# State-space layer on one core: 8 to 8.5 input tiles per group in place of 10, five gate tiles multiplied on at the end, decay rows over a group's x chunks, transposed sums

## The reference

```python
def ssd_chunked(x, dt, a, bm, cm, init_state):
    ...
    acs = jnp.cumsum(dtc * a.reshape(SSD_GROUPS, r), axis=2)
    seg = acs[:, :, :, None] - acs[:, :, None, :]
    lmat = jnp.exp(jnp.where(lower, seg, -jnp.inf))
    cb = jnp.einsum('bcign,bcjgn->bcijg', cc, bc)
    wmat = cb[..., None] * lmat * dtc[:, :, None]
    y_diag = jnp.einsum('bcijgr,bcjgrp->bcigrp', wmat, xc)
    ...
    chunk_states = jnp.einsum('bcjgn,bcjgrp->bcgrpn', bc, xw)
    ...
    y_off = jnp.einsum('bcign,bcgrpn->bcigrp', cc, starts) * jnp.exp(acs)[..., None]

def ssd_mixer(h, w_in, conv_w, conv_b, dt_bias, a_log, d_skip, norm_g, w_out, init_f=None, init_b=None):
    proj = h @ w_in
    z, xbc, dt = jnp.split(proj, [SSD_DI, SSD_DI + SSD_XBC_W], axis=-1)
    xbc = jax.nn.silu(dwconv_centered(xbc, conv_w, conv_b))
    ...
    y = y_f + jnp.flip(y_b, 1) + xs.astype(jnp.float32) * d_skip.astype(jnp.float32)[:, None]
    y = y.reshape(b, n, SSD_DI) * jax.nn.silu(z.astype(jnp.float32))
    y = rmsnorm(y, norm_g).astype(h.dtype)
    return y @ w_out, s_f, s_b
```

## Time and profile before

| | us |
|---|---|
| median of 3 runs | 1921.57 |
| lowest and highest | 1917.19, 1923.33 |
| profiled execution | 1917.99 |
| its span in the profile | 1916.2 |
| TensorE busy | 1830.8 |
| VectorE, ScalarE, GpSimdE busy | 999.6, 602.5, 1188.0 |
| TensorE busy from 1000 to 1050 us | 50.00 of 50 |
| from 1250 to 1300 us, granted clock 0.93 | 38.05 of 50 |
| from 1300 to 1350 us, granted clock 0.80 | 35.59 of 50 |

### The profile page before, as it was taken

The page is one execution under the profiler, slowest core; times in us unless marked ns, Lnnn a source line. Parts: engine busy times, 40 slices in busy tenths (PEclk is TensorE's granted clock), DMA queues, the critical chain, the costliest instruction groups (busy, mean ns, idle before and its releaser), DMA issues. The chain is left out here.

```text
span 1916.2 us, 33393 instructions
## 1 busy us (share of the span) xinstructions
PE 1830.8 (96%) x12837; PEld 1726.8 (90%) x12837; DVE 999.6 (52%) x1597; ACT 602.5 (31%) x1148; POOL 1188.0 (62%) x869
## 2 busy tenths in 40 slices
PE   6999999999999999989999999986999999999997
PEld 4888899999999999989898898965999999999997
DVE  4556654562256146373656756595436633661552
ACT  3344421220022012144566657473112200220221
POOL 2533466777777777846455454515787777777774
PEclk9999999999999999999999999997999999999999
DMA  9641164424243433534333333233222222222222
GB/s 342 198 136 38 32 223 151 157 75 155 67 164 92 139 102 115 166 92 135 99 111 111 99 111 99 67 100 110 67 78 66 77 76 67 77 77 72 71 61 82
DMA packets 256188, 208.65 MB, mean 109 GB/s; under 512 B 7353, under 2 KB 235742, under 8 KB 255454
## 3 DMA queue, kind: packets, MB, share of 16 engines
q1 hardware_dynamic: 255373, 204.69, 33.9%
q10 hardware_dynamic: 720, 2.62, 0.3%
HBM read 196.63 MB, written 10.67 MB: 108 GB/s over the span
## 5 line engine op out<-in xcount | busy, mean ns | idle before, releaser
L1002 POOL TENSOR_SCALAR w_hi<-raw 128x512 fp32r<-128x512 f32 (+1 forms) x432 | 641.0, 1501 | 706.7 <-PE ps L1036 527.2
L1006 POOL TENSOR_TENSOR w_lo<-raw,w_hi 128x512 fp32r<-128x512 f32 (+1 forms) x432 | 553.9, 1303 | 0.0
L1036 PE MATMUL ps<-h_hi,w_hi 128*128 128x324 f32 (+1 forms) x1432 | 343.8, 321 | 4.7 <-DVE h_lo L2392 3.1
L1036 PE MATMUL ps<-h_hi,w_lo 128*128 128x324 f32 (+1 forms) x1432 | 328.8, 311 | 0.0
L1036 PE MATMUL ps<-h_lo,w_hi 128*128 128x324 f32 (+1 forms) x1432 | 327.5, 310 | 0.0
L1036 PEld LDWEIGHTS ps<-h_hi,w_hi 128*128 128x128 f32 x1432 | 241.2, 190 | 20.7 <-issue 18.4
L1036 PEld LDWEIGHTS ps<-h_hi,w_lo 128*128 128x128 f32 x1432 | 240.5, 189 | 0.0
L1036 PEld LDWEIGHTS ps<-h_lo,w_hi 128*128 128x128 f32 x1432 | 240.3, 189 | 0.0
L2282 DVE SCALAR_TENSOR_TENSOR xT<-ps,mod,xT 128x128 f32 (+1 forms) x112 | 56.6, 547 | 270.9 <-PE ps L1036 265.3
L1036 PE MATMUL ps<-g_hi,w_hi 128*128 128x324 f32 (+1 forms) x816 | 188.7, 312 | 4.8 <-POOL w_lo L1006 3.2
L1036 PE MATMUL ps<-g_hi,w_lo 128*128 128x324 f32 (+1 forms) x816 | 187.2, 310 | 0.0
(11 more groups left out here) (355 smaller groups left out, 3113.7 us busy)
## 6 DMA issues: line engine op xcount, KB each, us to landing
raw<-in_ffn_w_up SPq DMA_DIRECT2D x88, 512.0 KB, 3.9
ada<-in_ada_w SPq DMA_DIRECT2D x40, 1024.0 KB, 6.5
raw<-in_ssd_w_in SPq DMA_DIRECT2D x40, 512.0 KB, 4.0
raw<-in_ffn_w_down SPq DMA_DIRECT2D x32, 512.0 KB, 3.9
R<-scr_acs SPq DMA_DIRECT2D x22, 512.0 KB, 5.3
raw<-in_att_w_in SPq DMA_DIRECT2D x16, 512.0 KB, 7.8
ada_att<-in_ada_w SPq DMA_DIRECT2D x8, 1024.0 KB, 8.3
raw<-in_ssd_w_out SPq DMA_DIRECT2D x16, 512.0 KB, 4.0
```

The source lines that it names most:

```text
L1002: nc.gpsimd.tensor_scalar(w_hi[j % 2][:, a_:b_, :], raw[j][:, a_:b_, :], 1.0, None, ALU.mult).then_inc(w_hi_done, 1)
L1006: ins = nc.gpsimd.tensor_tensor(w_lo[j % 2][:, a_:b_, :], raw[j][:, a_:b_, :], w_hi[j % 2][:, a_:b_, :].bitcast(F32), ALU.subtract)
L1036: ins = mm(out[:, cols], w[slot][:, k, :], x[:, cols], start=first and k == 0 and i == 0, stop=last and k == n - 1 and i == 2)
```

## The change

- **Tile order.** Groups 0 and 1 have 8 tiles (two z), group 2 has 9 (three z), group 3 has 10. The z tiles of rows 2, 3, 6, 7 and 11 stand at 35 to 39. Their rows of `yg` are set to 1 (five memsets in tile 3), the scan multiplies into them, and a new step `gate` on VectorE multiplies the SiLU of z, which ScalarE leaves in `cx`.
- **Scan places.** The b tiles are 0, 8, 16, 25 and the scans start at half tiles 14, 30, 47 and 64 (tiles 7, 15, 23.5 and 32).
- **End.** Chunks 0 to 3 of group 3 stand before the end of tile 39. Behind it follow `yd` of chunk 3, `yo` and `cb` of chunk 4, `yd` of chunk 4, then all out-projection pieces. `ynorm` is no longer spread through the scan.
- **Decay rows.** `R_last` lies over `x_tok[0]`, which group 2 has left, and its transfer waits for group 2 instead of tile 39.
- **Transposed sums.** The four matmuls at the end of `yd` are marked as transposes.
- **SyncE.** `LEAD` is 3. The store of `acs`, which SyncE waits for, now stands behind weight tile 7 where it stood behind tile 9. Two weight tiles of the out-projection are issued before the wait for the last `yd`.

```diff
+CONV_AT = (0, 8, 16, 25)
+SLOT_AT = (14, 30, 47, 64)
+Z_ROWS = ((0, 1), (4, 5), (8, 9, 10), (12, 13, 14, 15))
+Z_LATE = (2, 3, 6, 7, 11)
...
-        slots = [(b + 7 + i // 2, i % 2) for i in range(0, 40)]
+        slots = [divmod(SLOT_AT[g] + i, 2) for i in range(0, 40)]
...
-    return out
+        out += [ev for ev in after[k] if ev[0] != "yd"]
+    return out + end[:1] + [("yd", GROUPS - 1, 4)] + end[1:] + [("yout", GROUPS - 1, k) for k in range(12)]
...
-        R_last = at("R_last", [P, 2, GH, P], F32, aligned(h_at + 12 * WS * 4))[0]
+        R_last = x_tok[0][:, :, :].rearrange("p c n -> p (c n)")[:, 0:2 * GH * P].rearrange(
+            "p (a b c) -> p a b c", a=2, b=GH)
...
-                    sp.wait_ge(mm_done, T_E + 40)
+                    sp.wait_ge(*ssd_end(("yd", GROUPS - 2, CHUNKS - 1)))
+                    sp.wait_ge(st_done, CS_AT[("csf", GROUPS - 2, 3)] + 1)
...
-            LEAD = 5
+            LEAD = 3
...
-            sp.wait_ge(*ssd_end(("yd", 3, 4)))
-            sp.wait_ge(st_stored, 128)
-            sp.dma_start(xT[:, :, :], scr_x).then_inc(x_back, 16)
-            with sp.Fori(1, 4) as i:
+            for j in range(4):
+                if j == 2:
+                    sp.wait_ge(*ssd_end(("yd", 3, 4)))
+                    sp.wait_ge(st_stored, 128)
+                    sp.dma_start(xT[:, :, :], scr_x).then_inc(x_back, 16)
+                load(j, T_O + 4 + j, w_so[:, (j % 2) * 8:(j % 2) * 8 + 8, (2 + j // 2) * P:(3 + j // 2) * P])
+            with sp.Fori(2, 4) as i:
...
                         ins = mm(bank(b, P, q_ * P), y1[ev[2] % 2][:, q_ * P:(q_ + 1) * P], ident, start=False,
-                                 stop=q_ == 3, skip_group_check=True)
+                                 stop=q_ == 3, is_transpose=True, skip_group_check=True)
...
+                        if m in Z_LATE:
+                            dst = cx[:, :]
+                            if m != Z_LATE[0]:
+                                act.wait_ge(gated, Z_LATE.index(m))
+                        A_(dst, acc(e % 2), ACT.Silu).then_inc(acc_free_act, 1)
...
+                if kind == "gate":
+                    m = ev[2]
+                    dve.wait_ge(*acc_free(A_E + TILE_OF[("z", m)]))
+                    dve.wait_ge(*ssd_end(("yd", m // 4, 4)))
+                    tt(yg[:, m, :], yg[:, m, :], cx[:, :], ALU.mult).then_inc(gated, 1)
```

84 lines of the change are left out of this document (52 added, 32 removed).

## The result

The changed kernel takes 1947.63 us (median of four runs, 1945.96 to 1952.99) where the kernel before takes 1922.45 (four runs): a ratio of 1.0145, with a 95% interval of 1.0127 to 1.0163. It is slower, as forecast, but by 25 us where 15 were forecast: inside the range of 1908 to 1950, above the forecast's own of 1928 to 1944. The profiled execution took 1948.97 us, its span is 1947.2 us, its mean granted clock 0.973; before, these were 1917.99, 1916.2 and 0.985.

The account below looks back on a forecast made before the run. TensorE, busy 1830.8 of 1916.2 us, was taken as the bound. 1917.99 less 30.6 gained plus 48.2 added gave 1935.6, with half the 3.6 us offset about 1937 us; own range 1928 to 1944, wider range 1908 to 1950.

Parts of the forecast that it names:

- gain 3: Before the first regular out-projection tile: weights issued early save 2.2 of the 6.70 us wait.
- term 3: First `csb` of a group at tiles 15, 23 and 32 waits for VectorE's weighing: 4.7 us added in sum.
- Term 1: Half tiles 12.0 and 20.0: x transposes wait for a bank VectorE frees late, 7.2 us twice, 14.4 us added.
- Term 7: Low clock after the new waits of the x transposes: 2 us each, 6 us added together, bounds 0 and 9.
- term 6: Last chunk, between the last two `yd`: TensorE idle 5.1 us plus low clock 2.5, 7.6 us added.
- gain 1: Sums at the end of `yd` as transposes: 0.65 us saved 20 times, 13.1 us.
- Gain 2: Behind tile 39: the 5.39 us wait for `R_last` and the low clock behind it go, 8.5 us saved.
- Gain 4: The recurring bank waits of `cb` and `csf`, 3.8 and 3.0 us, are replaced by the added waits: 6.8 us saved.
- The rival in which each wait is at its floor: All added waits smallest, no low clock: 21.2 us added against 30.6 gained, 1910 us; chance 0.20.
- The rival of two passes: Sums in `yd` go through twice as before despite the transpose mark: 13.1 us more, 1950 us; chance 0.05.
- half and half: Bank waits some 4 us each, low clock behind only one: about 33 us added, 1920 to 1923 us; chance 0.17.
- the late tile 8: Weight tile 8 lands much later, behind other transfers: 1940 to 1943 us; chance 0.06.

Follow-up runs that it names:

- e3: The changed kernel with plain matmuls in place of transposes for the sums in `yd`: ratio 1.0197 to the kernel before.
- e1: The kernel before with only the sums at the end of `yd` marked as transposes: 1916.10 us, ratio 0.9979.
- e11: The changed kernel with another spacing, first group nine tiles long and group 2 eight: ratio 1.0176 to the kernel before.
- e2: The kernel before with only the last chunk's decay rows `R_last` laid over `x_tok[0]` and `ynorm`'s squares moved to `st_in`: ratio 0.9990.
- e12: The changed kernel with x transposes before `stT`, `acs` store and loads behind weight tile 9, first `csb` of groups 1 and 3 a half tile later: 1925.11 us, 1.0030.
- e4: The kernel before, old tile order, with transposed sums, decay rows over `x_tok[0]` and early loads of two out-projection weight tiles: 1915.34 us, ratio 0.9971.

## Why the prediction was right in sign and wrong in size

The sum was +17.6 us on the profiled execution; the stretch became 26.1 us longer. Taken apart into idle time, cheaper sums, and clock:

| | forecast | measured |
|---|---|---|
| idle time, net | +25.3 | +26.4 |
| transposed sums, busy time | -13.1 | -10.4 (e3) to -11.2 (e1) |
| low clock | +5.4 | +10.9 |

The forecast idle time is the added waits 1 to 6 and 8 without their low clock, 39.7, less the 5.39, 2.2 and 6.8 us of gains 2 to 4. The low clock measured is the busy time after less that of e1, 476.3 - 465.4: the same matmuls at different clocks. The forecast one is 6 + 2.5 - 3.1. Idle time and low clock are not quite separate costs, since where VectorE sets the pace the one takes from the other; their sum is what counts.

**The waits** were found at their places and nearly in their sizes (us):

| added | forecast | measured |
|---|---|---|
| 1. x transposes, twice | 14.4 | 13.3 |
| 2. the same at 28.1 and 29.0 | 5.3 | 5.4 (1.31 + 4.13) |
| 3. first `csb` of a group | 4.7 | 7.6 (3.95 + 0.80 + 2.82) |
| 4. half tiles 8.1, 16.1 | 4.7 | 4.7 |
| 5. weight tile 8 | 3.5 | 4.15 |
| 6. last chunk, without clock | 5.1 | 5.9 |
| 8. `yo` behind ScalarE | 2 | 1.4 |

These waits are 42.4 us where 39.7 were forecast, and the first wait for a split grew by 1.0 (gain 3 below). Against it, 2.8 us of short waits between 1267 and 1283 us in the kernel before went too, which no term had. So the net comes out 1.1 over the forecast.

Of term 3 the place at tile 32 was mis-sized, 0.5 us forecast for 2.82. Term 1 was right in its two legs as well: from the start of tile 10's convolution to the state update's end are 25.8 us (943.82 to 969.64) where the walk has 24.8, and TensorE's own work up to its request took about 1.7 us more than the walk's 17.6, in part by the low clock in it. The experiments took 1 (13.3 to 5.6 us), 3 (7.6 to 2.8) and 5 (to nothing) away and got that idle time back, so these causes are shown. Term 4 is shown for half tile 8.1 by e11, where it goes with a longer group. Terms 2, 6 and 8 have only their rows.

**What failed is the size of two terms.** Term 7, the low clock, was put at 2 us behind each of three long waits, term 6 had 2.5 us more, and the other waits had nothing. The trace shows it behind every one of the nine waits of 2.3 us or more ahead of the out-projection: the 10 us behind each read 0.82 to 0.84, after 2.34 us (921.07 and 1030.30) as after 4.15, 3.95 or 5.89. Eight of these waits are new and the ninth is that of term 6. A wait of 2.34 us cost about as much clock as one twice as long, so the number of waits was the thing to count, and the term came out twice as large. The profile of before had shown that short waits do it, in places that the walk did not read: the 10 us behind each of the three pairs of 1.28 and 0.99 us (949.38, 1059.00, 1168.61) read 0.83 to 0.85. One such row of before, from 1060 us on, reads 0.88, and this one, behind the pair a group earlier, 0.84:

```profile
950.00:960.00 10.00, 10.00 (x58) 9.14 (x56) 7.70 (x11) 2.71 (x4) 3.23 (x3) 0.84 0.18 54
```

And gain 1 was put at 0.65 us for each `yd`, as 1.09 less half of the 0.87 of an eight-transpose row (rows 3). A row of four transposes takes 0.66 us at full clock (980.36 in the changed kernel), not the 0.44 of the half. Over all 20 places the sums took 24.1 us before and 13.2 with transposes, that is 0.55 less each. Both errors go the same way, and with the waits' 1.1 they make 5.5 + 1.9 + 1.1 = 8.5 us, which is the miss in the stretch, 26.1 - 17.6. The profiled execution as a whole is 31.0 us longer; of the other 4.9, 2.8 lie ahead of the stretch, where kernels with the same work differ by as much, and 2.1 behind it, which no run explains.

**Gain 2** came true, but not by the part of the change that the expectation of e2 gave it to. The wait of 5.39 us stood before the `yd` of chunk 1. e2 shows that the place of the rows has no part in it: the row (rows 2) names VectorE's product as the releaser, and VectorE was late by its own steps. In the changed kernel that `yd` stands at 1263.95 without a wait, with input tiles' matmuls beside it; that the tiles are what took it off fits this but was not tried alone. A wait of the same kind, 5.89 us, stands before the last `yd` instead, where no tile is left, as term 6 said (5.1). **Gain 3** was right in its row (6.70 to 4.77), but the first of the three waits for a split grew from 6.07 to 7.07 and took half of it back. **Gain 4** holds: those two waits of rows 1 are gone.

The rival in which each wait is at its floor is out: its 3.8 us for the x transposes are 6.64. The rival of two passes is out by the 80 records, half and half by the 42 us of waits, and the late tile 8 by its 4.15 us. What the forecast missed as a possibility is that most of the slowness is not in the closeness of the groups as such: e12 has the same spacing and is 22 us faster. About 11 us to e4 are left, and how much of them the spacing costs is open.

## What to carry to other kernels

When two pipelined groups are moved closer, look at what now shares an issue slot, and put first the step whose inputs are oldest: one sort key gave 7.3 us, and one step a half tile later 8.9, while moving a whole group cost 9.7. Count idle time and low clock apart, and count the second behind every wait, short ones too. And before a wait is booked as gained, look at whether its releaser itself was waiting: in e2 the load came 3 us earlier for ScalarE, and TensorE waited for VectorE as long as before, because VectorE had been busy all along.
